# Merging the scores of two key blocks into 128 columns per head in a sliding-window attention layer

## The reference

```python
scores = einsum('bnqkgd,bnskd->bnkgqs', qb, kb) * HD ** -0.5   # 256 keys: previous block, current block
dist = qi[:, None] - kj[None, :] + BLK
mask = ((dist >= 0) & (dist < WINDOW)) & (kpos >= 0)           # WINDOW = 128
scores = where(mask, scores - slopes * dist, -inf)
m = maximum(scores.max(-1), sink)
e = exp(scores - m)
probs = e / (e.sum(-1) + exp(sink - m))
o = einsum('bnkgqs,bnskd->bnqkgd', probs, vb)
```

## Time and profile before

| what | us |
|---|---|
| median of three runs | 1123.49 |
| the profiled execution, its own time | 1123.27 |
| its span in the trace | 1121.5 |
| attention stage, from the first scores (block 0) to the last | 33.0 to about 282 |
| one block of it (scores of block 3 to scores of block 4) | 129.36 to 162.16 |

### The profile page before, as it was taken

How to read it: one execution, slowest core, us unless ns; L and a number is a source line. 1 busy time by engine, 2 the same in 40 slices (tenths; PEclk the granted TensorE clock), 3 DMA queues, 4 the chain that set the end, 5 groups by cost and what they waited for, 6 DMA issues and landing times.

```text
span 1121.5 us, 15068 instructions
## 1 busy us (share of the span) xinstructions
PE 1100.2 (98%) x5400; PEld 922.9 (82%) x5400; DVE 755.7 (67%) x1176; ACT 457.0 (41%) x808; POOL 111.1 (10%) x198
## 2 busy tenths in 40 slices
PE   7999999998999999999999999999999999999998
PEld 5788888887888888888888888888888888888886
DVE  6788877789553589876676667588777763664311
ACT  7566666677522334223313243453333331243100
POOL 6522232333000000000000000000000000010000
PEclk9999999999999999999999999999999999999999
DMA  7000000113152406444243153999888872111210
GB/s 263 20 20 19 19 0 19 37 47 141 39 169 75 150 1 212 165 152 166 113 188 149 78 202 141 387 412 309 294 291 286 290 256 75 38 38 57 85 47 37
DMA packets 61360, 153.87 MB, mean 137 GB/s; under 512 B 4720, under 2 KB 5752, under 8 KB 61304
## 3 DMA queue, kind: packets, MB, share of 16 engines
q1 hardware_dynamic: 61280, 153.12, 38.5%
q10 hardware_dynamic: 24, 0.01, 0.0%
HBM read 119.03 MB, written 34.08 MB: 137 GB/s over the span
## 4 chain that ended last, share of the span: by engine, by line
PE 78%; DVE 10%; ACT 5%; issue 4%; POOL 1%; DMA 1%; ACTq 0%; DVEq 0%; SPq 0%; POOLq 0%
PE pair L2145 24%; PE pair L2125 21%; PE pair L2188 8%; PE pair L1997 7%; PE pair L1860 4%; PE pair L2165 4%; PE pair L2083 3%; ACT probs L899 3%; PE pair L2201 2%; DVE probs L1331 2%; DVE probs L1349 2%; PE pair L1928 1%; PE pair L1899 1%; PE pair L2053 1%; DVE pT L1356 1%
## 5 line engine op out<-in xcount | busy, mean ns | idle before, releaser
L2145 PE MATMUL pair<-uT 128*128 128x512 f32 x1176 | 266.7, 389 | 0.0
L2145 PEld LDWEIGHTS pair<-uT 128*128 128x128 f32 x1176 | 220.7, 188 | 45.8
L1155 ACT ACTIVATE uT<-wo_raw 128x1024 fp32r<-128x1024 f32 x63 | 64.3, 1054 | 105.8 <-PE pair L2145 91.6
L1676 DVE TENSOR_TENSOR uT<-wo_raw,uT 128x1024 fp32r<-128x1024 f32 x63 | 74.9, 1221 | 39.3 <-ACT uT L1155 39.3
L1860 PE MATMUL pair<-WA,xT 128*128 128x512 f32 x384 | 95.7, 397 | 4.7 <-DVE WA L1254 3.4
L1997 PE MATMUL pair<-WA,oT 128*128 128x512 f32 x384 | 90.1, 392 | 0.6 <-DVE oT L1437 0.3
L1860 PEld LDWEIGHTS pair<-WA,xT 128*128 128x128 f32 x384 | 69.6, 188 | 21.6 <-issue 6.5
L1997 PEld LDWEIGHTS pair<-WA,oT 128*128 128x128 f32 x384 | 71.2, 188 | 15.3 <-DVE rmax L1331 0.5
L899 ACT ACTIVATE probs<-probs,nmax 128x257 f32<-128x257 f32 x128 | 63.7, 500 | 48.4 <-DVE nmax L1336 48.2
L2125 PE MATMUL pair<-WA,WB 128*128 128x512 f32 x336 | 78.2, 389 | 0.4 <-ACT xr L1130 0.4
L668 POOL TENSOR_SCALAR row_var<-row_ssq 128x1 f32<-128x1 f32 x16 | 3.0, 191 | 720.0 <-ACT hn L1054 720.0
(11 more groups left out here) (194 smaller groups left out, 1934.7 us busy)
## 6 DMA issues: line engine op xcount, KB each, us to landing
wo_raw<-in_m_w SPq DMA_DIRECT2D x53, 512.0 KB, 6.5
wo_raw<-hid_kept SPq DMA_DIRECT2D x36, 512.0 KB, 4.7
hid_kept<-RES SPq DMA_DIRECT2D x28, 512.0 KB, 2.7
emb<-in_m_w SPq DMA_DIRECT2D x20, 512.0 KB, 6.4
RES<-in_m_w SPq DMA_DIRECT2D x8, 1024.0 KB, 7.2
uT_f<-in_m_w SPq DMA_DIRECT2D x6, 1024.0 KB, 6.8
act_buf<-hid_kept SPq DMA_DIRECT2D x11, 512.0 KB, 4.7
hn<-in_m_w SPq DMA_DIRECT2D x11, 512.0 KB, 5.9
```

The lines of the kernel that those rows point to most:

```text
L1155: nc.scalar.activation(operand(t, which, HI), unit(t, which), ACT.Copy).then_inc(op_hi, 1)
L1676: nc.vector.tensor_tensor(operand(t, which, LO), unit(t, which), operand(t, which, HI).bitcast(F32), ALU.subtract).then_inc(op_ready, 1)
L2145: mm = nc.tensor.matmul(ps[4 * (j % 2) + m][:], operand(t, 0, s)[:, k, m * P:(m + 1) * P], operand(t, 1, r)[:, k, :], start=(g == 0 and k ...
```

## The change

The scores stay 256 columns wide in PSUM. Then DVE copies, for each pair of columns, the current block's score over the previous block's one where a 0/1 triangle `current` is set (two `copy_predicated` per group, one for each bank), and all that follows works on 128 columns per head: the bias, the exponentials, the scaling (now one `tensor_tensor` over the four heads, with the reciprocals broadcast), four transposes in place of eight, one high and one low part of 512 columns in place of two. `bias` and `probs` shrink; unnamed filler tensors keep the places of the others.

The output is then sum(p · v_current) over all columns plus sum(p · (v_previous − v_current)) over the columns that belong to the previous block. For the second sum POOL makes masked copies of the transposed probabilities (`mask_probs`: two `affine_select` of 512 columns per group), DVE the difference of the values (`v_diff`), POOL a copy of it in place of `shift_v` (`dv_hi_part`), DVE a second low part in `v_lo_part`, and POOL keeps the values for the next block (`keep_v`). PE still does 12 matmuls per group, with the current half first. POOL's two low parts of `wo` go to DVE. In the beginning POOL makes the triangle and a merged `dist` in place of the memset of `bias`.

```diff
+        score_keys = [bank.rearrange("p (h a n) -> p h a n", h=2, a=2) for bank in score_bank]
...
-            def shift_v(b):
-
-                stand(pool, pv_done, 4 * b)
-                copy(vz[:, 0], vz[:, 1]).then_inc(v_shifted, 1)
...
+            def dv_hi_part(b):
+
+                stand(pool, v_diffed, b + 1)
+                if not (isinstance(b, int) and b == 0):
+                    stand(pool, pv_done, 4 * b)
+                copy(vz[:, 0, HI, HD:(2 * KV + 1) * HD].rearrange("p (v a d) -> p v a d", v=KV, a=2)[:, :, 0, :],
+                     vprev[:].rearrange("p (v d) -> p v d", v=KV)).then_inc(dv_moved, 1)
+
+            def keep_v(b):
+                stand(pool, v_ready, 2 * b + 2)
+                copy(vprev[:], vnext[:]).then_inc(dv_moved, 1)
+
+            def mask_probs(t):
+
+                stand(pool, pT_hi, t + 1)
+                pool.affine_select(out=pT[:, HI, 0, :], in_=pT[:, HI, 1, :].bitcast(F32), compare_op=ALU.is_gt, fill=0.0,
+                                   base=0, pattern=[[0, G], [-1, P]], channel_multiplier=1).then_inc(pT_masked, 1)
+                stand(pool, pT_ready, t + 1)
+                pool.affine_select(out=pT[:, LO, 0, :], in_=pT[:, LO, 1, :].bitcast(F32), compare_op=ALU.is_gt, fill=0.0,
+                                   base=0, pattern=[[0, G], [-1, P]], channel_multiplier=1).then_inc(pT_masked, 1)
...
             def body(n, last=False):
                 head_norm("q8", n)
                 place_sinks(n, 1)
-                place_sinks(n, 2)
-                if last:
-
-                    pool.wait_ge(probs_ready, 4 * n + 1)
-                    wo_lo_unit(WO_POOL[0])
-                shift_v(n)
-                if last:
-                    wo_lo_unit(WO_POOL[1])
+                mask_probs(4 * n - 1)
                 if not last:
                     x_norm(n + 1)
+                place_sinks(n, 2)
+                if not last:
                     head_norm("q0", n + 1)
+                dv_hi_part(n)
+                mask_probs(4 * n)
+                if not last:
+                    keep_v(n)
                 place_sinks(n, 3)
                 if not last:
                     head_norm("k", n + 1)
+                mask_probs(4 * n + 1)
+                if not last:
                     shift_k(n + 1)
                     place_sinks(n + 1, 0)
+                mask_probs(4 * n + 2)
...
-                    row = probs[:, i, r, 0:2 * P + 1]
+                    row = probs[:, i, r, 0:P + 1]
...
-            def pT_hi_part(t):
-
-                for kt in range(2):
-                    act.wait_ge(probs_turned, 2 * t + (1 + kt))
-
-                    wait(act, pv_done, t)
-                    nc.scalar.activation(pT[:, HI, kt, :], pT_bank[kt][:], ACT.Copy).then_inc(pT_hi, 1)
+            def pT_hi_part(t, odd):
+
+                act.wait_ge(probs_turned, t + 1)
+
+                wait(act, pv_done, t)
+                nc.scalar.activation(pT[:, HI, 1, :], pT_bank[odd][:], ACT.Copy).then_inc(pT_hi, 1)
...
+            def v_diff(b):
+                dve.wait_ge(v_staged, b + 1)
+                if isinstance(b, int) and b == 0:
+                    dve.wait_ge(zeros_ready, 3)
+                wait(dve, dv_moved, 2 * b)
+                nc.vector.tensor_tensor(vprev[:], vprev[:], vnext[:], ALU.subtract).then_inc(v_diffed, 1)
...
+                dve.wait_ge(dv_moved, 2 * b + 1)
+                nc.vector.tensor_tensor(values(0, LO), vprev[:].rearrange("p (v d) -> p v d", v=KV),
+                                        values(0, HI).bitcast(F32), ALU.subtract).then_inc(v_ready, 1)
 
             def add_bias(n, j, first):
...
+                for half_bank in range(2):
+
+                    stand(dve, scores_ready, 2 * t + (1 + half_bank))
+                    nc.vector.copy_predicated(score_keys[half_bank][:, :, 0, :],
+                                              current[:].bitcast(U32).unsqueeze(1).to_broadcast([P, 2, P]),
+                                              score_keys[half_bank][:, :, 1, :]).then_inc(wrapped, 1)
                 for r in range(G):
...
                     nc.vector.tensor_tensor_reduce(
-                        probs[:, i, r, 0:2 * P], score_bank[r // 2][:, (r % 2) * 2 * P:(r % 2 + 1) * 2 * P],
+                        probs[:, i, r, 0:P], score_keys[r // 2][:, r % 2, 0, :],
                         bias[:, G * j + r, :], 1.0, 0.0, ALU.add, ALU.max, rmax[:, i, r:r + 1]).then_inc(biased, 1)
...
-                for r in range(G):
-                    ts = nc.vector.tensor_scalar(probs[:, i, r, 0:2 * P], probs[:, i, r, 0:2 * P], rden[:, i, r:r + 1],
-                                                 None, ALU.mult)
-                ts.then_inc(probs_ready, 1)
+                nc.vector.tensor_tensor(probs[:, i, :, 0:P], probs[:, i, :, 0:P],
+                                        rden[:, i, :].unsqueeze(2).to_broadcast([P, G, P]),
+                                        ALU.mult).then_inc(probs_ready, 1)
...
-                wait(pe, pT_ready, 2 * t)
-                for kt in range(2):
-                    for r in range(G):
-                        mm = nc.tensor.transpose(pT_bank[kt][:, pos(r) * P:(pos(r) + 1) * P],
-                                                 probs[:, j % 2, r, kt * P:(kt + 1) * P], ident[:])
-                    mm.then_inc(probs_turned, 1)
+                wait(pe, pT_ready, t - 1)
+                for r in range(G):
+                    mm = nc.tensor.transpose(pT_bank[j % 2][:, pos(r) * P:(pos(r) + 1) * P],
+                                             probs[:, j % 2, r, 0:P], ident[:])
+                mm.then_inc(probs_turned, 1)
...
-                pe.wait_ge(pT_ready, 2 * t + 2)
-                pe.wait_ge(v_ready, n + 1)
+
+                pe.wait_ge(pT_ready, t + 1)
+                pe.wait_ge(v_ready, 2 * n + 1)
 
                 wait(pe, attended, t)
                 done = 0
-                for kt in range(2):
+                for kt in (1, 0):
+                    if kt == 0:
+                        pe.wait_ge(pT_masked, 2 * t + 2)
+                        pe.wait_ge(v_ready, 2 * n + 2)
```

More of the change, by code:

```diff
@@ L25 @@
 F32R = mybir.dt.float32r
+U32 = mybir.dt.uint32
 ALU = mybir.AluOpType
@@ L32 @@
 EPS = 1e-6
-WO_DVE, WO_POOL = (0, 1, 4, 5, 6, 7), (2, 3)
 WARM_UP = 34
@@ L151, in trunk_layer @@
         pT = sb("pT", [P, 2, 2, BANK], F32R, in_a)
-        probs = sb("probs", [P, 2, G, 2 * P + 2], F32, in_a)
-        bias = sb("bias", [P, H, 2 * P], F32, in_a)
+        probs = sb("probs", [P, 2, G, P + 2], F32, in_a)
+        vprev = sb("vprev", [P, KV * HD], F32, in_a)
+        current = sb("current", [P, P], F32, in_a)
+        sb("after_probs", [P, 640], F32, in_a)
+        bias = sb("bias", [P, H, P], F32, in_a)
+        sb("after_bias", [P, H * P], F32, in_a)
         dist = sb("dist", [P, 2 * P], F32, in_a)
@@ L347, in trunk_layer @@
         v_staged = sem("v_staged")
-        v_shifted = sem("v_shifted")
+        v_diffed = sem("v_diffed")
+        dv_moved = sem("dv_moved")
         v_hi = sem("v_hi")
@@ L658, in _ @@
             pool.memset(half[:], -0.5).then_inc(half_ready, 1)
-            pool.memset(ident[:], 0.0).then_inc(ident_zero, 1)
-            pool.wait_ge(ident_zero, 1)
+            pool.memset(ident[:], 0.0).then_inc(ident_ready, 1)
+            pool.wait_ge(ident_ready, 1)
             pool.affine_select(out=ident[:], in_=ident[:], compare_op=ALU.not_equal, fill=1.0,
@@ L689, in _ @@
             pool.memset(kT[:].bitcast(F32), 0.0).then_inc(zeros_ready, 1)
+            pool.memset(vprev[:], 0.0).then_inc(zeros_ready, 1)
+            pool.memset(current[:], 1.0).then_inc(current_ready, 1)
+            pool.wait_ge(current_ready, 1)
+            pool.affine_select(out=current[:], in_=current[:], compare_op=ALU.is_ge, fill=0.0,
+                               base=0, pattern=[[-1, P]], channel_multiplier=1).then_inc(current_ready, 1)
             pool.iota(dist[:], pattern=[[-1, 2 * P]], base=P, channel_multiplier=1,
@@ L693, in _ @@
             pool.wait_ge(dist_step, 1)
-            pool.affine_select(out=dist[:], in_=dist[:], compare_op=ALU.is_ge, fill=-1e3 * MASKED,
+            pool.affine_select(out=dist[:], in_=dist[:], compare_op=ALU.is_ge, fill=0.0,
                                base=P, pattern=[[-1, 2 * P]], channel_multiplier=1).then_inc(dist_step, 1)
             pool.wait_ge(dist_step, 2)
-            pool.affine_select(out=dist[:], in_=dist[:], compare_op=ALU.is_ge, fill=-1e3 * MASKED,
+            pool.affine_select(out=dist[:], in_=dist[:], compare_op=ALU.is_ge, fill=0.0,
                                base=-1, pattern=[[1, 2 * P]], channel_multiplier=-1).then_inc(dist_step, 1)
             pool.wait_ge(dist_step, 3)
+            pool.tensor_tensor(dist[:, 0:P], dist[:, 0:P], dist[:, P:2 * P], ALU.add).then_inc(dist_step, 1)
+            pool.wait_ge(dist_step, 4)
```

(37 more changed lines are left out.)

64 lines of the change are left out of this document (29 added, 35 removed).

## The result

The changed kernel takes 1117.14 us (median of 6 runs, 1116.91 to 1118.67) against 1123.6 us before: a ratio of 0.9947 (95% interval 0.9934 to 0.9959). It is faster, by 6.5 us in place of the 14.6 forecast, and outside the range. The profiled execution took 1118.16 us, 5.1 less than the one of before.

A forecast was written before the change was run, and what follows sets the result against it. PE, busy 32.21 of 32.80 us a block, was the bound, with the chain to the normed keys 0.14 us behind. Blocks 1 to 6 give 10.8, block 0 0.2, block 7 3.6: 14.6 us, so 1108.9 us, range 1106.5 to 1111.

The forecast's parts named there:

- PE's own work: Attention blocks on PE: four of eight transposes per group go, 0.43 us a group, 1.7 us per block.
- floor of a block: Period of an attention block without PE waits: 32.80 - 0.55 - 1.72 = 30.53 us.
- The softmax, per group: DVE and ACT in each group: DVE's sum -0.8 us, hidden beside PE except where it is on the chain.
- POOL's new work: Two masks per group at 0.62 us each; POOL rises from 9.3 to some 14 of 31 us a block.
- slower rivals: copy_predicated at its upper bound: 1112.5, chance 0.10; POOL becomes the bound through masks of 2.75 us or more: 1130, chance 0.05.
- The chain to the normed keys: From turn_q of q8 to the normed keys: -0.65 us in sum, PE waits about 0.5 us a block, period 31.0.
- first rival: POOL's first mask goes ahead of DVE's second low part of v: 0.62 us on the chain, 1113, chance 0.23.
- Block 0: First attention block: add_bias holds PE, +0.25; normed keys no earlier; -0.43 in group 3; gain 0.2 us.
- detour over POOL: DVE's second low part of v waits for dv_hi_part, behind head_norm of q0 on POOL: 0.57 + 1.65 + 0.50 us.
- late add_bias: In block 0 add_bias, longer by the new copies, holds PE twice: +0.25 us.
- Block 7: Last attention block: 1.7 us from transposes plus half of PE's waiting; gain 3.6 us.
- Of PE's 4.0 us of waiting I take back half: Block 7: half of PE's waits go, as ACT's 1.26 us wait for POOL goes and DVE saves 3.2 against 2.6.

The follow-up runs named there:

- first experiment: Changed kernel with the high part of the value difference ahead of head_norm of q0 on POOL: 1106.97 us, ratio 0.9853.
- second experiment: Changed kernel with place_sinks of group 3 between the high part of the value difference and POOL's first mask: 1112.51 us, ratio 0.9896.
- last two experiments: First experiment with low parts 2 and 3 of wo back on POOL: 1106.03 us; first experiment with DVE making those parts in another order in block 7: 1104.61 us.
- third: Changed kernel with the low parts 2 and 3 of wo back on POOL: 1116.44 us, ratio 0.9932.
- fourth experiment: Changed kernel with 16 unused transposes on PE in block 7, after the scores of group 2: 1114.46 us, ratio 0.9919.

## Why the prediction was wrong

The forecast against the profiled execution's own time was 1108.7, and it took 1118.16: 9.5 us off. By its own steps:

- **PE's own work**: right. 0.35 in place of 0.79 us per turn_probs. The floor of a block, forecast at 30.53 us, is 30.24 (first experiment, no wait left).
- **The softmax, per group, and POOL's new work**: right in every size that I had bounded: copy_predicated 0.33 a step (0.34), scaling 0.69 (0.68), a mask 0.64 (0.62). POOL is busy 14.0 us of a block (14). No PE wait for masks, none of the slower rivals.
- **The chain to the normed keys**: the step that named the new wait was right, in place and in kind: the second low part of v waits 1.24 us for POOL behind the root of q0, and PE waits for the normed keys. It was mis-sized: 0.5 us was forecast for PE, 1.15 measured. 0.4 of that is the mask that starts 0.08 us ahead of DVE, the first rival, which is what happened (second experiment): I gave it a chance of 0.23 and a price of 0.62, and the forecast itself put it at nothing; 0.3 is that PE's floor lies lower, so that PE arrives earlier. I had held against this rival that DVE starts within 0.05 us of a release and POOL some 0.1 after its last operation. But POOL's operations overlap in the records: dv_hi_part is recorded at 144.34 for 0.41 us, and the mask starts at 144.70, inside it. The trace before had that too: the root of q0 at 145.57 takes 1.65 us, to 147.22, and POOL's next operation starts ahead of that, at 147.19. Blocks 1 to 6 gave 8.0 us in place of 10.8: 2.8 of the 9.5.
- **Block 0**: forecast -0.2, measured +2.2. Two things failed. The detour over POOL was counted in blocks 1 to 6 and put at nothing here, though block 0 has it too:

```profile
48.98 0.83 DVE L1363 TENSOR_TENSOR vz<-vprev,vz 128x256 fp32r<-128x256 f32 x1 [1.45 <-POOL vz L737]
```

  It gave PE the new wait of 1.32 us before turn_q. Of the late add_bias I had a part (PE waits 1.02 before the scores of group 1, from 0.44, 0.6 more where I had 0.25), and the wait of 1.03 for the normed keys stayed, as I had it. And a wait was taken to cost its own length: PE stood 1.32 + 1.04 us and fell to 1.2 GHz. With filler in those waits block 0 was 31.3 us, 1.65 less; without the detour, in the last two experiments, it was 29.5 and 29.6.
- **Block 7**: forecast -3.6, measured +0.8. Two terms failed. "Of PE's 4.0 us of waiting I take back half" was no working, only a share (and 1.7 and 2.0 are 3.7): ACT's wait of 1.26 us for POOL did go, but the two wo parts on DVE stand in front of PE's third piece, and PE still stands 4.8 us (0.46, 0.66, 1.10, 2.06, 0.19 and 0.30). Without the half clock the block is 38.0 us, a gain of 1.8 in place of 3.6. The other 2.6 are the clock.

So of 9.5 us, 4.2 are a clock that was 1.00 in all of the trace before and of which the prediction had no term, 2.8 the chain, and 2.5 the rest of blocks 0 and 7. Without the clock this execution would have taken 1113.9 us, inside the range and near the first rival's 1113; its being so near is in part luck, as the rival had 3.4 us from blocks 0 and 7, which without the clock gave 1.2.

What stays open is what makes the clock fall: why in block 7 of the changed kernel and not in the first experiment, where that block runs the same program with the same waits, and why one program loses it in some executions and keeps it in others. No run here settles that.

## What to carry to other kernels

When a value gets a second producer, put it ahead of everything on its engine that it does not need: here one copy stood behind a reciprocal root that it had nothing to do with, and moving it was worth more than the change without it (10.2 us against 6.5 by the medians; blocks 0 to 6, which the move touches, became 11.0 us shorter). When an engine is nearly full, list each wait that a change gives it in any block, first and last ones too: a wait on TensorE can cost more than its length. Where DVE reads two SBUF tensors behind an event of POOL's, reckon with POOL's next SBUF operation getting in first, as it did here in blocks 0 to 6. And look at the granted clock of every execution before giving an edit credit for 1 or 2 us.

## What was not expected of the hardware

TensorE's granted clock went to 0.50 after standing 1.32 and 1.04 us with only four transposes between: 0.50 from 57 to 60 us, and 0.99 again from 60 to 63. It did so in block 0 of all four traces that have two such waits there without filler (the changed kernel and the second, third and fourth experiment; 0.75 and 1.04 us in the second), and not in the four that have only the one for the normed keys (1.03 before, 0.75 to 0.79 with the difference first); in block 3 one wait of 1.15 us left it at 1.00. In block 7 it fell in two traces and stayed in two others with the waits of 1.10 and 2.06 us, one of which had filler in the second wait. The same program showed it in some executions and not in others, with times up to 2.7 us apart. In the first experiment it was also below 1.00 in the set-up (0.90 from 0 to 33 us), where the others were at 1.00.

A DVE instruction of 256 columns with two SBUF inputs took 0.83 us when POOL's mask had started 0.08 us before it, and 0.42 or 0.43 without; the scaling in block 7, with two SBUF inputs as well, took 0.92 in place of 0.69 beside a mask.
